# Attention's output projection cut into two parts by heads, with half units of it inside the last attention steps

## The reference

```
def _diff_attention(xm, k_all, v_all, ...):
    q = _rms((xm @ w_q).reshape(B, T, A_HEADS, 2, A_DH), q_g) * (A_DH ** -0.5)
    ...
    p = jax.nn.softmax(jnp.where(mask, s + bias, NEG_BIG), axis=-1)
    a = p[:, :, 0] - lam * p[:, :, 1]
    o = jnp.einsum('bhqk,bkhe->bqhe', a, v_all)      # by blocks of queries
    o = _rms(o, head_g) * (1 - lam_init)
    return (o.reshape(B, T, D_MODEL) @ w_o).astype(xm.dtype)
...
x = x + g1[:, None, :] * y
xm = _modulate(x, p['norm_g'][l, 1], sh2, sc2)
x = x + g2[:, None, :] * _swiglu(xm, p['ffn_w_gate'][l], p['ffn_w_up'][l], p['ffn_w_down'][l])
```

## Time and profile before

| | us |
|---|---|
| median of 3 runs (lowest to highest) | 1564.32 (1562.94 to 1566.42) |
| profiled execution: its time, its span | 1569.69, 1567.9 |
| PE busy / weight loads busy | 1510.9 (96%) / 1424.1 (91%) |
| DVE, ACT, POOL busy | 842.2, 416.5, 748.9 |
| mean granted TensorE clock | 0.98 |

### The profile page before, as it was taken

One profiled execution on the slowest core, in us unless ns is written; L12 is line 12 of the kernel. 1 busy time (PEld: TensorE's weight loads), 2 busy tenths in 40 slices (PEclk: granted clock), 3 DMA queues, 4 the chain that ended last, 5 costly groups with the idle time before them and its releaser, 6 DMA issues.

```text
span 1567.9 us, 31755 instructions
## 1 busy us (share of the span) xinstructions
PE 1510.9 (96%) x12494; PEld 1424.1 (91%) x12494; DVE 842.2 (54%) x1499; ACT 416.5 (27%) x894; POOL 748.9 (48%) x456
## 2 busy tenths in 40 slices
PE   5999999999999999999999989988899999999998
PEld 4998898999999999999997867767899999999998
DVE  6503455454342134445573167765557579557587
ACT  4302454221110011112211146665321123111132
POOL 2445333455454455554444423443455556455554
PEclk8999999999999999999999989977999999999999
DMA  9455413433536234343322332220122222222222
GB/s 363 129 174 166 133 68 109 153 131 122 197 142 235 88 122 187 134 166 128 99 71 67 95 135 83 83 76 21 54 81 80 82 89 88 91 81 80 85 93 98
DMA packets 53928, 183.49 MB, mean 117 GB/s; under 512 B 6232, under 2 KB 8672, under 8 KB 53584
## 3 DMA queue, kind: packets, MB, share of 16 engines
q1 hardware_dynamic: 51136, 174.63, 33.1%
q10 hardware_dynamic: 2704, 7.64, 1.3%
HBM read 171.69 MB, written 10.55 MB: 116 GB/s over the span
## 4 chain that ended last, share of the span: by engine, by line
PE 89%; DVE 5%; ACT 3%; issue 2%; DMA 0%; ACTq 0%; POOL 0%; SPq 0%; DVEq 0%; POOLq 0%
PE psum L656 61%; PE psum L702 7%; PE psum L898 7%; PE psum L667 3%; PE psum L1067 2%; PE psum L904 1%; PE psum L1120 1%; PE psum L1016 1%; PE psum L1107 1%; PE psum L997 1%; PE psum L805 1%; PE psum L1080 1%; PE psum L1150 1%; PE psum L834 1%; PE psum L1135 1%
## 5 line engine op out<-in xcount | busy, mean ns | idle before, releaser
L557 POOL TENSOR_SCALAR w_hi<-raw 128x1024 fp32r<-128x1024 f32 (+1 forms) x168 | 189.9, 1130 | 618.2 <-PE psum L656 495.0
L656 PE MATMUL psum<-act_hi,w_hi 128*128 128x288 f32 (+1 forms) x2048 | 448.2, 300 | 5.9 <-POOL w_lo L559 3.0
L656 PE MATMUL psum<-act_lo,w_hi 128*128 128x288 f32 (+1 forms) x2048 | 442.1, 297 | 0.0
L656 PE MATMUL psum<-act_hi,w_lo 128*128 128x288 f32 (+1 forms) x2048 | 442.0, 297 | 0.0
L559 POOL TENSOR_TENSOR w_lo<-raw,w_hi 128x1024 fp32r<-128x1024 f32 (+1 forms) x168 | 433.5, 2581 | 14.0
L656 PEld LDWEIGHTS psum<-act_hi,w_hi 128*128 128x128 f32 x2048 | 332.2, 190 | 12.0 <-issue 9.0
L656 PEld LDWEIGHTS psum<-act_hi,w_lo 128*128 128x128 f32 x2048 | 332.4, 190 | 0.0
L656 PEld LDWEIGHTS psum<-act_lo,w_hi 128*128 128x128 f32 x2048 | 331.9, 190 | 0.0
L656 PE MATMUL psum<-hid_both,w_hi 128*128 128x288 f32 x704 | 122.7, 297 | 0.0
L656 PEld LDWEIGHTS psum<-hid_both,w_hi 128*128 128x128 f32 x704 | 103.6, 189 | 0.6 <-issue 0.6
L1725 DVE SCALAR_TENSOR_TENSOR x<-psum,mod,x 128x288 f32 (+2 forms) x96 | 34.2, 412 | 99.9 <-PE psum L656 98.7
(11 more groups left out here) (320 smaller groups left out, 2222.3 us busy)
## 6 DMA issues: line engine op xcount, KB each, us to landing
raw<-in_w_stream SPq DMA_DIRECT2D x153, 512.0 KB, 3.5
ada_quad<-in_ada_w SPq DMA_DIRECT2D x48, 512.0 KB, 5.2
raw<-in_w_down SPq DMA_DIRECT2D x32, 704.0 KB, 4.2
ada_ring<-in_ada_w SPq DMA_DIRECT2D x32, 512.0 KB, 4.4
ada_first<-in_ada_w SPq DMA_DIRECT2D x8, 1024.0 KB, 15.7
line_rep<-line SPq DMA_DIRECT2D x8, 352.0 KB, 4.5
line<-line_rep SPq DMA_DIRECT2D x8, 352.0 KB, 5.3
x<-in_x SPq DMA_DIRECT2D x4, 576.0 KB, 5.8
```

The source lines that it names most:

```text
L557: pool.tensor_scalar(hi, src, 1.0, 0.0, ALU.mult, ALU.add).then_inc(hi_split, 1)
L656: last = mm(psum[:, b + half, 0:n_cols], weights[wp][:, k, :], parts[ap][:, k, half * HT:half * HT + n_cols], start=(k == 0 and n == 0), s ...
```

## The change

The eight output units are cut another way: a unit is now two output tiles (a pair) over four heads: `OUT_PARTS[n]` = (pair, part), part 0 heads 0 to 3, part 1 heads 4 to 7. The first three units (part 0 of pairs 0, 1, 2) need only heads 0 to 3, and are used in quarters of 12 matmuls, one output tile by one half of T (`out_part(f)`, f = 0 to 11). Quarters 0 to 6 stand at the end of steps 36 to 42, quarter 7 after the loop, then head 7's `att_sums`, then 8 to 11. Quarters 0 to 7 all write bank 7, and each waits (`o_half_read`) until DVE has added the one before to `x` (`part_to_x`); quarters 8 to 11 stay in banks 0 to 3 and are added to by unit 5. Units 3 to 7 are then done tile by tile (`out_tile`). Their residual (`out_residual`) adds tile m to `x` first and makes the low part and the square sum of tile m-1 after it. From head 6 on, the mean squares of tiles 1 and 3 stand behind the step's transposes and values, on PE and on ACT. SP loads a unit as two runs of 512 columns (`load_out`), in the same places of its queue. POOL's instructions are the same.

```diff
+OUT_PARTS = ((0, 0), (1, 0), (2, 0), (0, 1), (1, 1), (2, 1), (3, 0), (3, 1))
...
+        o_half_mm, o_half_read, o_done, o_x = sem("o_half_mm"), sem("o_half_read"), sem("o_done"), sem("o_x")
...
+            def load_out(n):
+
+                pair, part = OUT_PARTS[n]
+                u, m, c = U_AO + n, stream_index(U_AO) + 2 * pair, 512 * part
+                sp.wait_ge(lo_split, u - 1)
+                sp.dma_start(raw[:, u % 2, 0:KT * P].rearrange("p (u n) -> p u n", u=2),
+                             w_stream[m:m + 2, :, c:c + 512].rearrange("u p n -> p u n")).then_inc(raw_in[u % 2], 16)
...
-                load_unit(U_AQ + 2 + h)
+                load_unit(U_AQ + 2 + h) if h < H - 2 else load_out(h - (H - 2))
...
-            load_unit(U_AO + 2)
-            load_unit(U_AO + 3)
-            load_pairs(U_AO + 4, 2)
+            for n in range(2, 8):
+                load_out(n)
...
+                    pe.wait_ge(at_ready, 5 * n - 6 + late)
...
+                pe.wait_ge(at_ready, min(5 * H, 5 * h + 6 + late))
...
-            def out_step(k):
-
-                pe.wait_ge(lo_ready[A_O], k + 1)
-                for j in range(2):
...
+            def out_part(f):
+
+                n, c = divmod(f, 4)
+                u, j, half = U_AO + n, c // 2, c % 2
+                pe.wait_ge(lo_split, u + 1)
+                if f == 0:
+                    pe.wait_ge(evac[(U_AQ + 7) % 2], (U_AQ + 7) // 2 + 1)
+                    pe.wait_ge(lo_ready[A_O], 4)
+                elif n < 2:
+                    pe.wait_ge(o_half_read, f)
+                elif c == 0:
+                    pe.wait_ge(scored, 5 * H)
+                for k in range(4):
+                    for i, (wp, ap) in enumerate(SPLIT3):
+                        last = mm(psum[:, 7 if n < 2 else c, 0:HT], w_parts[u % 2][wp][:, 4 * j + k, :],
+                                  act[BUF[A_O]][ap][:, k, half * HT:(half + 1) * HT],
+                                  start=(k == 0 and i == 0), stop=(n < 2 and k == 3 and i == 2))
+                if c == 3:
+                    last.then_inc(unit_done, 1)
+                elif n < 2:
+                    last.then_inc(o_half_mm, 1)
+
+            def out_tile(n, j, k, bank, start, last_k=False):
+
+                u, part = U_AO + n, OUT_PARTS[n][1]
+                for i, (wp, ap) in enumerate(SPLIT3):
+                    for half in range(2):
+                        last = mm(psum[:, bank + half, 0:HT], w_parts[u % 2][wp][:, 4 * j + k, :],
+                                  act[BUF[A_O]][ap][:, 4 * part + k, half * HT:(half + 1) * HT],
+                                  start=(start and i == 0), stop=(last_k and i == 2))
+                return last
...
+            parts = iter(range(12))
...
+                late = p >= H - 2
...
-                if g >= 5 * H:
-                    if s == 0:
-                        pe.wait_ge(scored, 5 * H)
-                        for j in range(2):
-                            pe.wait_ge(lo_split, U_AO + j + 1)
-                            wait_evac(pe, U_AO + j)
-                    out_step(s)
-            for k in range(3, KT):
-                if k == 4:
-                    att_sums(H - 1)
-                    att_sums_sample(H - 1)
-                out_step(k)
-            def o_pair(i):
-                project(U_AO + 2, i, act[BUF[A_O]])
-                project(U_AO + 3, i, act[BUF[A_O]])
-            loop(pe, 3, o_pair)
+                if s == 1 and p == H - 2:
+                    query_sums(p + 1)
+                    query_sums_sample(p + 1, late=True)
+                elif s == 3 and late:
+                    att_sums(p - 1)
+                    att_sums_sample(p - 1, late=True)
+                if g > 5 * H - 5:
+                    out_part(next(parts))
+            out_part(next(parts))
+            att_sums(H - 1)
+            att_sums_sample(H - 1)
+            for f in parts:
+                out_part(f)
+            pe.wait_ge(lo_split, U_AO + 4)
+            pe.wait_ge(o_half_read, 8)
+            pe.wait_ge(o_out, H)
+            pe.wait_ge(oz_ready, H)
+            for k in range(4):
+                pe.wait_ge(lo_ready[A_O], 5 + k)
+                out_tile(3, 0, k, 4, k == 0, k == 3).then_inc(o_done, 1) if k == 3 else out_tile(3, 0, k, 4, k == 0)
+                last = out_tile(3, 1, k, 6, k == 0, k == 3)
+            last.then_inc(unit_done, 1)
+            for n, banks in ((4, 4), (5, 0)):
+                pe.wait_ge(lo_split, U_AO + n + 1)
+                for j in range(2):
+                    if n == 4:
+                        pe.wait_ge(o_x, j + 1)
+                    for k in range(4):
+                        last = out_tile(n, j, k, banks + 2 * j, n == 4 and k == 0, k == 3)
+                    last.then_inc(unit_done if j else o_done, 1)
+            pe.wait_ge(lo_split, U_AO + 7)
+            for j in range(2):
+                pe.wait_ge(o_x, j + 3)
+                for k in range(4):
+                    last = out_tile(6, j, k, 4 + 2 * j, k == 0)
+            last.then_inc(unit_done, 1)
+            pe.wait_ge(lo_split, U_AO + 8)
+            for j in range(2):
+                for k in range(4):
+                    last = out_tile(7, j, k, 4 + 2 * j, False, k == 3)
+                last.then_inc(unit_done if j else o_done, 1)
...
+            def feed(u0, norm, feeds, ready=None):
                 def pair(i):
                     for j in range(2):
-                        sa.wait_ge(evac[(u0 + j) % 2], i + ((u0 + j) // 2 + 1))
+                        if ready:
+                            sa.wait_ge(ready, i * 2 + (j + 1))
+                        else:
...
+                late = p >= H - 2
...
+                if s == 1 and queries and not late:
-                elif s == 3 and out:
+                elif s == 3 and out and not late:
                 att_exp(g)
+                if s == 1 and queries and late:
+                    query_z(p + 1)
+                elif s == 3 and late:
+                    z_sample(p - 1)
...
-            feed(U_AO, N_FFN1, [(A_FFN1, gain_of(3))])
+            feed(U_AO, N_FFN1, [(A_FFN1, gain_of(3))], ready=o_x)
...
+            def part_to_x(f):
+                n, c = divmod(f, 4)
+                m, half = 2 * n + c // 2, c % 2
+                if c == 3:
+                    ve.wait_ge(unit_done, U_AO + n + 1)
+                else:
+                    ve.wait_ge(o_half_mm, 3 * n + c + 1)
+                for h, a0, a1, g in parts3:
+                    if h == half:
+                        xs = x[:, m, half * HT + a0:half * HT + a1]
+                        last = stt(out=xs, in0=psum[:, 7, a0:a1], scalar=mod[:, 8 * (LAYER + GATE_A) + m, g:g + 1], in1=xs,
+                                   op0=ALU.mult, op1=ALU.add)
+                last.then_inc(o_half_read, 1)
+            def out_residual():
+                for m in range(KT + 1):
+                    if m < KT:
+                        if m % 2 == 0:
+                            ve.wait_ge(o_done, m // 2 + 1)
+                        else:
+                            ve.wait_ge(unit_done, U_AO + (4, 5, 6, 8)[m // 2])
+                        bank = (4, 4, 0, 4)[m // 2] + 2 * (m % 2)
+                        for half, a0, a1, g in parts3:
+                            xs = x[:, m, half * HT + a0:half * HT + a1]
+                            last = stt(out=xs, in0=psum[:, bank + half, a0:a1], scalar=mod[:, 8 * (LAYER + GATE_A) + m, g:g + 1],
+                                       in1=xs, op0=ALU.mult, op1=ALU.add)
+                        last.then_inc(o_x, 1)
+                        if m in (4, 5):
+                            ve.wait_ge(o_x, m + 1)
+                            ve.sem_inc(evac[m - 4], 4)
+                    if m > 0:
+                        ve.wait_ge(o_x, m)
+                        scaled_lo(A_FFN1, gain_of(3), m - 1)
+                        acc_tile(N_FFN1, m - 1)
+                     att_score(g)
+                if g > 5 * H - 4:
+                    part_to_x(g - (5 * H - 3))
                     att_weight(g - 1)
+            for f in range(4, 6):
+                part_to_x(f)
             head_lo(H - 2)
+            for f in range(6, 8):
+                part_to_x(f)
-            residual(U_AO, LAYER + GATE_A, N_FFN1, [(A_FFN1, gain_of(3))])
+            out_residual()
```

25 lines of the change are left out of this document (7 added, 18 removed).

## The result

The changed kernel takes 1558.7 us in the median of 8 runs (1555.38 to 1563.13), the kernel before, beside it, 1567.99 (8 runs, 1562.94 to 1570.64): ratio 0.9946, 95% interval 0.9929 to 0.9964, so 8.5 us or 0.54% off, between 5.6 and 11.1. The forecast was 16.5 us off, 1547.8 from a base of 1564.3. The profiled execution took 1563.13 us, with a span of 1561.1. It is faster, as forecast, by about half as much.

The account below looks back on a forecast made before the run. The prediction took PE, 89% of the chain, as the bound, losing time in waits and at half clock. Its terms, 14.0 - 0.5 - 1.8 + 0 + 4.8 = 16.5 us, took 1564.3 to 1547.8 us; range 1543 to 1557.

Parts of the forecast that it names:

- point 5: Head 6 without the stall in step 31: gain 4.8 us, or 6.3 if the clock holds.
- point 4: Steps 36 to 42: added quarters 6.3 us and bank 7 waits 1.8, against 8.5 of room; about 0.
- point 3: Quarter 7, waiting behind head 6's low part and quarter 6's reading, delays head 7's sums: loss 1.8 us.
- points 1 and 2: Output units after head 7's sums: gain 14.0 us; wait for tile 0's residual: loss 0.5 us.
- point 2: Unit 4 waits for tile 0's residual: loss 0.5 us; last tiles' work before the FFN is covered, costing nothing.
- Point 6: Loads of output units as two 512-column runs: 0 us, each landing before its cut may begin.
- steps pay for the quarters: Rival, chance 0.26: clock stays low well into head 7, quarters run at half speed; gain only 11.8 to 7.3 us.
- clock 0.50 in steps 36 to 40: Sign that the forecast is wrong: PE at half clock in steps 36 to 40.
- quarters 1 to 3 waiting over 1 us each: Sign that the forecast is wrong: these quarters' waits exceed 1 us each, where 0.6 each was forecast.
- Bank 7 becomes the chain: Rival, chance 0.05: eight quarters each hold PE 2.5 us or more longer over bank 7; slower, 1568 us.

Follow-up runs that it names:

- the experiment above: Changed kernel plus 12 unused dense matmuls at the end of each of steps 31 to 35 (60 in all): 1555.68 us, ratio 0.9922 to the kernel before.
- readings first: Changed kernel with DVE's score tile and its reading of bank 7 exchanged in steps 37 to 40, reading first: 1553.15 us, ratio 0.9909 to the kernel before.
- both readings: Changed kernel with bank 7 read before the score tile in steps 37 to 40, and quarter 6 read before head 6's low part: 1555.11 us, ratio 0.9914.
- units alone: Changed kernel with mean squares in their old order and no quarters in steps 36 to 39: 1565.43 us, ratio 0.9978 to the kernel before.
- order alone: Kernel before with only the mean squares moved behind transposes and values in heads 6 and 7, on PE and ACT: 1565.69 us, ratio 0.9976.

## Why the prediction was right or wrong

Set against the traces: the region took 117.1 us in the trace that I worked from and 105.4 after, a gain of 11.7 (11.2 between the means of three and of two traces); the prediction had 16.5. By points it is 5.8 for point 5, -3.2 for point 4, -2.8 for point 3 and 11.9 for points 1 and 2.

*Point 5, head 6: right.* Forecast 4.8 with bounds to 6.3; 5.8 against the trace that I worked from, 4.3 against the mean of three (26.2 to 21.9). Head 6 came into the forecast band: 21.85 us with 3.4 us at half clock in it, each time. The wait before the sums of step 31 is gone; part of it is back as 1.97 us before step 32's transposes, for DVE (L2185).

*Point 4, steps 36 to 42: this step failed,* and the term that failed is the clock. The sum took 4.7 us off because "the quarters are" dense enough for the full clock. Instead 10.24 us at half clock lay at the seam, from the end of step 35 through quarter 0, in both traces of the changed kernel: the transposes and values of step 36 and quarter 0 itself ran at 0.50 (quarter 0 took 2.88 us, not 1.6). The quarters came too late to prevent it; dense work already in steps 31 to 35 did (the experiment above). From head 6's fifth score tile to the end of step 39's values it took 35.9 us where the trace I worked from had 32.65: 3.2 us lost where 0 was forecast. That is the clock's price, by three comparisons: the short stretch of 6.8 us in "readings first" made the way to step 37's scores 3.1 us shorter; "both readings", with the long one, took 3.3 more in head 7 for the same instructions; and with dense work in head 6 and no half clock at all those steps took 32.85 us, the loop over bank 7 and 12 useless matmuls included. The 4.7 us themselves were counted from a stretch (1078.45 to 1088.65) that the kernel before, repeated, had for only 3.4 us in one execution and for far longer in the other.

The waits in point 4 were right, partly by luck. It said 0.6 us each for quarters 1, 2 and 3, 1.8 in all, and the exchange shows the hand-over to be worth 1.8 to 2.0 us. But the waits themselves are 0.21, 0.64 and 0.64, 1.5 in all; what they don't show is that a quarter behind a wait takes 1.83 instead of 1.59, and that each step goes once around through PE and DVE, 5.1 us against 4.27 without the loop. I had looked at each queue for what the wait holds up on its own engine, and not followed the loop back; so I did not see that two instructions in the other order take it away.

*Point 3, quarter 7: right mechanism, too small.* From the last values to the sums it took 1102.86 - 1096.66 = 6.2 us against 3.4: a loss of 2.8 instead of 1.8. The wait is the one forecast, 2.12 us behind head 6's low part and quarter 6's reading. The term left out the half clock that came behind this wait: quarter 7 took 2.31 instead of 1.60, and the sums behind it 2.03 instead of about 1.0.

*Points 1 and 2, the units: right.* From the sums to the last output matmul 53.35 us before, 1144.32 - 1102.86 = 41.46 after: 11.9 against 13.5 forecast. About 1.3 of the shortfall are the half clock just named. PE's one wait in it is the 0.53 us for tile 0's residual, as point 2 had it. GpSimd's splits of the third and fourth units came 3.2 us later than the sum put them (1092.6, 1099.9), like the work around them, and ended 5.5 and 4.9 us before PE needed them:

```profile
1095.85 1.04 POOL L568 TENSOR_SCALAR w_hi<-raw 128x1024 fp32r<-128x1024 f32 x1 [0.44 <-POOL kt_sb L612]
1096.97 2.38 POOL L570 TENSOR_TENSOR w_lo<-raw,w_hi 128x1024 fp32r<-128x1024 f32 x1
1103.06 1.04 POOL L568 TENSOR_SCALAR w_hi<-raw 128x1024 fp32r<-128x1024 f32 x1 [3.70 <-PE psum L1168]
1104.18 2.38 POOL L570 TENSOR_TENSOR w_lo<-raw,w_hi 128x1024 fp32r<-128x1024 f32 x1
```

The cover at the FFN's start held only just: DVE's last piece ended at 1149.96, and PE's first matmul that needs it came at 1150.00. Tile 6's low part took 3.09 us instead of 0.94 there, beside a split by GpSimd, which point 2 had not counted:

```profile
1145.33 3.09 DVE L1773 SCALAR_TENSOR_TENSOR act_lo<-x,gain,act_hi 128x512 fp32r<-128x512 f32 x2
...
1145.62 2.71 POOL L570 TENSOR_TENSOR w_lo<-raw,w_hi 128x1024 fp32r<-128x1024 f32 x1
```

*Point 6: right.* No wait for a load.

*Whether the terms of the sum are independent is not shown.* By ratio the units alone give 3.5 us, the order alone 3.8, and the quarters 3.9 on top of the units (0.9978 to 0.9953): 11.2 together, while the whole change gives 8.5. On top of units and quarters the order brings 1.1, and on top of units and order the quarters 0.3. That points to order and quarters filling the same idle time. But with intervals of 2 to 3 us either way to each of these ratios a difference of 2.7 is not clear of noise, and in the traces the clock is mixed in: without the quarters head 7 took 18.05 us with the short stretch at the seam, with them 24.7 with the long one.

*The rivals.* The gain of 8.5 us lies within the 7.3 to 11.8 of "steps pay for the quarters" (two or three quarters at 1.6 are 3.2 to 4.8, not 0 to 4.5, so its range should have been 7.0 to 8.6). That rival named the place and the cause: the clock stayed low over 10.25 us at the seam, though it slowed one quarter, not two or three. The sign of being wrong "clock 0.50 in steps 36 to 40" came too; "quarters 1 to 3 waiting over 1 us each" did not come. "Bank 7 becomes the chain" described the loop; it cost 1.8 to 2.0 us in all and not 2.1 a quarter, but its case against was the very thing that made it: that the reading stands directly behind the score tile. The Trainium skill, "TensorE: Matmul & The Clock Gate", Part 1, is not borne out in its bare form (the clock returns once the engine is busy): 37.5 us with PE busy for 34.96 stayed at 0.50. PE's busy time doesn't tell the two levels apart: with the dense work it was busy for 22.46 of 24.00 us, as large a share, at 1.00. As for VectorE and GpSimd, the split of the fourth unit (1103.06 to 1106.56) and head 7's normalization on DVE (from 1107.28) missed each other; where the two did meet is told in the last section.

*What stays open.* The region gained 11.2 us by traces and the whole kernel 8.5 by ratio (5.6 to 11.1), so up to 2.7 lie ahead of it, in code that is the same but for the load of the first output unit. The fifth score tile of head 5 stands at 1034.1 to 1036.2 in four traces with the code of before up to there and at 1033.8 to 1039.4 in ten of changed kernels, 1.6 later in the mean; the late ones have one or two more stretches of 3.4 us at half clock, near 268 and 912 us, as has one of the four. Whether that is chance in so few traces, or the changed kernels bring it about, no run tells. Nor is it settled why head 6, with the same order of PE's work, took 24.7 to 27.7 us in the three traces of before and 23.9 and 24.2 in two of changed kernels.

## What to carry to other kernels

Don't book a gain from the full clock because the work slipped in is dense: look at what TensorE does ahead of it. Here the half clock began in the sparse steps before the first quarter, and cost 3.1 us. Before costs are taken from one trace, look at a second one for whatever depends on the clock.

When two traces differ, find the first instruction at which they part. If it lies ahead of the first edited one, the edit did not cause it: of 6.2 us that seemed to come of one exchange, about 2 did.

When work is handed over through one buffer inside a loop, write down the round trip (producer, what is queued behind it, what the consumer does before it reads) and compare it with the step. Put the read that frees the buffer first on the consumer's engine; it cost nothing here and gave about 2 us.
